# Moving one block's query work: its start put three experts earlier, two contraction steps behind each expert

## The chip, the cores and the metric

The program runs on one core of one Trainium2 chip. The metric is device time in microseconds (us) of one execution. The kernel before takes 1707.67 us (median of 3 runs, 1706.31 to 1708.52). A core has a matrix engine (PE; its weight load is PEld), a vector engine (DVE), a scalar engine (ACT), a general engine (POOL, which here issues the indirect gathers) and SP, which issues the other transfers. All data are float32.

## What is computed

One step of a hybrid decoder for 512 prompt tokens and 64 sample tokens: a token mixer (windowed attention and a spatial gate), a cross attention to memory tokens, and a mixer that picks experts by product keys. The last one takes nearly all of the time. Per token and head it is, cut to what matters:

```python
q = (xt @ w_pq).reshape(PEER_BLOCK, PEER_HEADS, 2, D_HALF)
s = jnp.einsum('thcd,hckd->thck', q, sub_keys)
s1, i1 = lax.top_k(s[:, :, 0], 16)
s2, i2 = lax.top_k(s[:, :, 1], 16)
cand = s1[..., :, None] + s2[..., None, :]          # 16 x 16 pairs
top, sel = lax.top_k(cand, 16)
idx = take_along_axis(i1 * 128 + i2, sel)
gate = softmax(top)
h = einsum('td,thkd->thk', xt, u_tab[idx])
a = gelu(h) * gate
out = einsum('thk,thkd->td', a, v_tab[idx])
```

With 16384 experts of 1024 + 1024 numbers each, every token reads 8 x 16 rows of 8 KB from memory.

## The kernel before

The 576 rows of tokens (64 sample tokens as tile 0, then four tiles of 128) times 8 heads are cut into 36 **blocks** of 128 (token, head) pairs: blocks 0 to 3 hold tile 0 with two heads each, blocks 4 to 11 the first prompt tile, and so on. A block has 16 **experts**, one chosen row per partition each. They are numbered g = 16 x block + k, from 0 to 575; block 4 begins at g = 64.

An expert passes through five engines:

- POOL gathers its 128 rows of 8 KB (1.05 MB) into one of the slots of scratch memory (line 641). Each slot goes round: the gather waits until the expert that held the slot before has been used by PE (`v_used`). A table in the kernel (`SLOT_PHASES`) says which slots take part. Worked out from it, for the experts that the text speaks of: gather 48 takes the slot of expert 40, gather 53 that of 45, 58 that of 50, 64 that of 56, 65 that of 57, 66 that of 58, and 70 that of 63. Before the first gather of a block POOL also waits for that block's indices (`idx_ready`).
- DVE takes the dot product with the tokens (line 1462), once the gather has landed.
- ACT does three small operations (lines 911, 915 and 920): Gelu, times the gate, and a diagonal matrix of the result. Here they are called the diagonal of expert g.
- PE multiplies the diagonal with the second half of the gathered rows into accumulators (line 2009), and so frees the slot.

Each engine's program is one loop over g, in which other work is written between the experts by tables of numbers. An engine never skips an item that has to wait; everything behind it waits too. Two kinds of this other work matter here.

**Query work of a block** (`query_steps`): a counter `step` runs from the block's `query_at` on, one step an expert. Steps 0 to 7 are the 8 contraction steps of the query projection on PE (line 1802), at step 9 ACT copies the sum (`queries_out`, line 811) and PE transposes it (1812), at 11 ACT copies that (815) and PE computes the scores (1823), at 13 ACT copies them (821), at 15 and 16 DVE takes the 16 best of each half (`top_keys`, lines 1284 to 1288), at 18 the 16 best pairs (`best_pairs`, 1302 to 1305), at 20 the expert indices (`experts_of`, 1309 to 1324, after which POOL may gather for that block), at 21 ACT computes the exponentials of the gates (826), at 23 DVE scales them (1329). For a block s `query_at` is (s - 2) x 16, plus `LATE`. For a block in `QUICK` steps 0 to 7 come two at a time behind four experts, and all later steps four experts sooner.

**Units** (`UNIT_AT`): the windowed attention of the prompt tiles 2 to 4, in six pieces u = 0 to 5 that begin at experts 24, 31, 38, 44, 51 and 57. Offsets count from that start: PE scores at 0 (1958), DVE maxima at 4 (1397 to 1404), ACT exponentials at 5 (891), PE transposes at 6 (1971), ACT copies at 8 (897), PE values at 9 (1978), DVE scaling at 12 (1416). Of the odd ones ACT takes a sum of squares and a root at 13 (902, 903), DVE scales the rows at 16 (1268, 1269), PE transposes at 18 (1831) and DVE takes that at 21 (`attn_take`, line 1274). The transposes of unit 3 (at expert 50) wait for the `attn_take` that belongs to unit 1 and stands in DVE's program at expert 52; those of unit 5 (at expert 63) for that of unit 3, at expert 65.

At experts 77 and later the output projection and the next tile's work follow. SP reloads two tiles of the prompt (2 x 512 KB) when expert 59 has been used.

Of the kernel before, what the change touches and what calls it, by code (L numbers as in the profile page):

```python
# [110 lines left out]
def hybrid_step(nc, I, O):  # L111
    ctx = ExitStack()
    with ctx:
# [307 lines left out]
        UNIT_AT = (24, 31, 38, 44, 51, 57)  # L421
        OUT_AT = (77, 81, 85, 91, 95, 99, 105, 109, 113, 119, 123, 127)

        LATE = {4: 8, 12: 7}
        QUICK = (12,)

        def query_at(s):

            return (s - 2) * TOPK + LATE.get(s, 0)

        def query_steps(g):

            steps = []
            for s in range(BLOCKS):
                d = g - query_at(s)
                if s in QUICK and 0 <= d < KD // 2:
                    steps += [(s, 2 * d), (s, 2 * d + 1)]
                elif s in QUICK and KD // 2 <= d < 2 * TOPK:
                    steps.append((s, d + KD // 2))
                elif s not in QUICK and 0 <= d < 2 * TOPK:  # L440
                    steps.append((s, d))
# [1632 lines left out]
```

## Time and profile before

| | |
|---|---|
| time, median of 3 runs | 1707.67 us |
| the profiled execution's own time | 1707.81 us |
| its span | 1706.0 us |
| busy: PE, DVE, ACT, POOL | 1301.5, 1165.7, 810.4, 641.3 us |
| DMA queue of the gathers | 604.28 MB, 85.7% of 16 engines |
| mean over the span | 385 GB/s |
| first and last gather issued | 206.0 and 1676.0 us |

The profile is one execution. Its span leaves out 1.8 us of the execution's own time. A slice of the span (42.65 us each) shows 408 GB/s in the eighth, 374 in the ninth and 420 or more in most others.

### The profile page before, as it was taken

Reading aid. Unit: us, or ns where it says so; the run is one execution under the profiler, and the core shown is the slowest. Engines: PE = TensorE matmul, PEld = TensorE weight load, DVE = VectorE, ACT = ScalarE, POOL = GpSimd, SP = SyncE. Lnnn points to the kernel's source line nnn. Section 1 sums busy time; section 2 is a strip of 40 time slices with the busy share of each in tenths; the row PEclk is TensorE's granted clock in tenths of the full one; section 3 lists DMA queues with packets and bytes.
Section 4 is the critical chain, followed back from the end, with each engine's and each line's share of the span. In section 5 each row is a group of like instructions: output and inputs, shape, how many; then the busy total and the mean of one; then the engine's idle time right before and its main releaser. Section 6 shows DMA issues by size and latency. Waiting matters only on the chain.

```text
span 1706.0 us, 21619 instructions
## 1 busy us (share of the span) xinstructions
PE 1301.5 (76%) x7069; PEld 475.1 (28%) x7069; DVE 1165.7 (68%) x2795; ACT 810.4 (48%) x2337; POOL 641.3 (38%) x584
## 2 busy tenths in 40 slices
PE   9999878987889776677777776776767677667665
PEld 4455523433444222122322111111111111111110
DVE  2544578887667677787777777777667677677764
ACT  1434366775444354455555454445444445444443
POOL 0000044434434344444444443444444444444441
PEclk9999998899999988899988777878888877888866
DMA  9433699999999999999999999999999999999995
GB/s 353 168 138 134 232 400 422 408 374 422 421 421 421 420 398 420 421 403 421 419 421 412 422 421 421 421 422 421 421 421 421 421 405 422 421 421 420 422 419 220
DMA packets 99041, 657.35 MB, mean 385 GB/s; under 512 B 12576, under 2 KB 17568, under 8 KB 22368
## 3 DMA queue, kind: packets, MB, share of 16 engines
q0 software_dynamic: 83056, 604.28, 85.7%
q1 hardware_dynamic: 15872, 51.68, 8.1%
q8 instruction: 56, 0.92, 0.2%
q14 instruction: 57, 0.47, 0.1%
HBM read 652.71 MB, written 4.19 MB: 385 GB/s over the span
## 4 chain that ended last, share of the span: by engine, by line
DMA 44%; PE 26%; ACT 11%; DVE 10%; issue 7%; POOL 2%; ACTq 0%; DVEq 0%; SPq 0%; POOLq 0%
DMA R<-in_peer_uv,R 43%; PE ps L2009 10%; PE ps L1543 6%; DVE R L1462 4%; PE ps L1802 3%; ACT L911 2%; ACT R L920 2%; PE ps L1515 2%; ACT R L915 1%; POOL R L641 1%; ACT R L911 1%; ACT L826 1%; DVE R L1285 1%; DVE R L1286 1%; DVE R L1288 1%
## 5 line engine op out<-in xcount | busy, mean ns | idle before, releaser
L2009 PE MATMUL ps<-R 64*64 64x512 f32 x4536 | 732.3, 725 | 370.4 <-ACT R L920 364.9
L641 POOL DMA_INDIRECT R<-in_peer_uv,R x567 | 627.8, 1107 | 966.4 <-PE ps L2009 762.8
L1462 DVE CUSTOM_DVE_ANT_0 R<-R 128x1024 f32<-128x1024 f32 x567 | 689.3, 1225 | 382.4 <-DMA R<-in_peer_uv,R 368.3
L911 ACT ACTIVATE R<-R 128x1 f32<-128x1 f32 x576 | 115.9, 201 | 594.6 <-DVE R L1462 585.2
L2009 PEld LDWEIGHTS ps<-R 64*64 64x64 f32 x4536 | 134.5, 149 | 713.3 <-ACT R L920 627.1
L920 ACT ACTIVATE R<-R 128x64 f32<-128x64 f32 x576 | 200.4, 348 | 54.3 <-ACT R L915 1.5
L1802 PE MATMUL ps<-A,R 128*128 128x256 f32 (+1 forms) x640 | 224.8, 479 | 0.7 <-ACT R L802 0.7
L915 ACT ACTIVATE R<-R 128x1 f32<-128x1 f32 x576 | 169.8, 295 | 21.2 <-ACT R L911 0.4
L1802 PEld LDWEIGHTS ps<-A,R 128*128 128x128 f32 (+1 forms) x640 | 96.3, 201 | 261.9 <-issue 260.4
L1543 PE MATMUL ps<-A,R 128*128 128x512 f32 (+1 forms) x256 | 101.1, 547 | 0.0
L911 ACT ACT_TABLE_LOAD x60 | 77.0, 1283 | 9.0 <-DVE R L1462 8.0
L1515 PE MATMUL ps<-R 128*128 128x256 f32 (+2 forms) x352 | 78.7, 377 | 0.0
L1515 PEld LDWEIGHTS ps<-R 128*128 128x128 f32 x352 | 60.1, 200 | 23.2 <-issue 16.1
L1543 PEld LDWEIGHTS ps<-A,R 128*128 128x128 f32 x256 | 47.6, 191 | 43.7 <-issue 41.8
L1462 DVE DVE_READ_ACCUMULATOR2_ANT R<- 128x1 f32 x576 | 47.6, 83 | 0.0
L826 ACT ACT_TABLE_LOAD x35 | 44.9, 1283 | 0.6
L1287 DVE MAX8 R<-R 128x8 f32<-128x128 f32 (+1 forms) x108 | 36.7, 339 | 3.7
L1284 DVE MAX8 R<-R 128x8 f32<-128x128 f32 (+1 forms) x108 | 36.3, 336 | 1.9 <-ACT R L821 0.5
L1285 DVE FIND_INDEX8 R<-R 128x8 uint32<-128x128 f32 (+1 forms) x108 | 35.6, 330 | 0.0
L1288 DVE FIND_INDEX8 R<-R 128x8 uint32<-128x128 f32 (+1 forms) x108 | 35.6, 330 | 0.0
L1286 DVE MATCH_REPLACE8 R<-R 128x128 f32<-128x128 f32 (+1 forms) x108 | 34.6, 320 | 0.0
L1823 PEld LDWEIGHTS ps<-R 128*128 128x128 f32 (+1 forms) x160 | 22.0, 209 | 38.2 <-issue 36.6
(288 smaller groups left out, 936.6 us busy)
## 6 DMA issues: line engine op xcount, KB each, us to landing
R<-in_peer_uv,R POOLq DMA_INDIRECT x567
A<-in_w_pq SPq DMA_DIRECT2D x8, 1024.0 KB, 10.3
A<-in_w_in SPq DMA_DIRECT2D x3, 2048.0 KB, 20.5
R<-in_w_out SPq DMA_DIRECT2D x5, 1024.0 KB
x_res<-in_x_prompt SPq DMA_DIRECT2D x6, 512.0 KB, 12.9
R<-in_w_out SPq DMA_DIRECT2D x1, 3072.0 KB
R<-in_x_promptT SPq DMA_DIRECT2D x4, 512.0 KB, 9.2
R<-in_w_cq SPq DMA_DIRECT2D x2, 1024.0 KB, 10.9
```

What stands on the lines that cost most here:

```text
L641: pool.indirect_dma_start(slots[slot_of[g]], None, I["peer_uv"][:, :], bass.IndirectOffsetOnAxis(ap=idx[:, b % 4, k:k + 1], axis=0)).then_ ...
L826: act.activation(gate[:, m, :], bestv, ACT.Exp, bias=negtop, accum_out=esum).then_inc(gexp_ready, 1)
L911: act.activation(hgelu[:, b % 2, col], hdot[:, b % 2, col], ACT.Gelu).then_inc(gelu_ready, 1)
L915: act.activation(coef[:, b % 2, col], gate[:, b % 4, col], ACT.Copy, scale=hgelu[:, b % 2, col])\
L920: act.activation(diag[:, g % DIAGS, :], fold[:, 0:HALF], ACT.Copy, scale=coef[:, b % 2, col])\
L1285: chain(dve.max_index(inds[:, 0:8], vals[:, 0:8], values))
L1288: return dve.max_index(inds[:, 8:16], vals[:, 8:16], values)
L1462: dve.tensor_tensor_reduce(u, u, xn(t), 1.0, 0.0, ALU.mult, ALU.add, hdot[:, b % 2, k:k + 1]).then_inc(u_used, 1)
L1515: ins = pe.matmul(out, lhs(k), rhs(k), start=(k == 0), stop=(k == n - 1))
L1543: ins = pe.matmul(bank(c)[:, 0:CHUNKS[c][1] - CHUNKS[c][0]], tile_T(t)[:, k, :], w_in[c][:, k, :], start=(k == 0), stop=(k == KD - 1))
L1802: ins = pe.matmul(bank(4)[rows, 0:256], expert_T(t)[:, k, :], w_pq(h)[:, k, :], start=(k == 0), stop=(k == KD - 1))
L2009: ins = pe.matmul(bank(2 * (t % 2) + q)[rows], diag[tokens, g % DIAGS, :], v_rows[slot_of[g]][tokens, c * 512:(c + 1) * 512], start=first, ...
```

## The change

```diff
-        LATE = {4: 8, 12: 7}
-        QUICK = (12,)
+        LATE = {4: 5, 12: 7}
+        QUICK = (4, 12)
```

`query_at(4)` goes from 40 to 37, and block 4 joins the blocks whose contraction steps come in pairs. So its steps 0 to 7 stand behind experts 37 to 40 instead of 40 to 47, and each later step stands seven experts sooner: the ACT copies at 42, 44 and 46 instead of 49, 51 and 53; top keys at 48 and 49 instead of 55 and 56; best pairs at 51 instead of 58; indices at 53 instead of 60; the gates' exponentials at 54 instead of 61. The work of no other block moves, the number and kind of instructions stay, and POOL's and SP's programs are the same.

PE's program around experts 37 to 40. L2009 is an expert, L1958 the scores of unit 2, L1978 the values of unit 1, L1802 a contraction step of block 4's queries:

```order
 L2009 MATMUL ps<-R 64x512 x4
+L1802 MATMUL ps<-A,R 128x256 x2
 L1958 MATMUL ps<-R 128x256 x4
-L2009 MATMUL ps<-R 64x512 x8
+L2009 MATMUL ps<-R 64x512 x4
+L1802 MATMUL ps<-A,R 128x256 x2
+L2009 MATMUL ps<-R 64x512 x4
+L1802 MATMUL ps<-A,R 128x256 x2
 L1978 MATMUL ps<-R 128x64 x8
 L2009 MATMUL ps<-R 64x512 x4
-L1802 MATMUL ps<-A,R 128x256
```

Six contraction steps now stand ahead of expert 40, where none stood; two more follow it.

ACT's program of the changed kernel around expert 42. L911, L915 and L920 are a diagonal, L891 and L893 the exponentials of unit 2, L811 the copy of block 4's queries and L815 that of their transpose:

```order
L915 ACTIVATE R<-R 128x1
L920 ACTIVATE R<-R 128x64
L811 ACTIVATE gather<-ps 128x256
L911 ACTIVATE R<-R 128x1
L915 ACTIVATE R<-R 128x1
L920 ACTIVATE R<-R 128x64
L911 ACTIVATE R<-R 128x1
L915 ACTIVATE R<-R 128x1
L920 ACTIVATE R<-R 128x64
L891 ACT_TABLE_LOAD
L891 ACTIVATE R,stat<-R,stat 128x256 x4
L893 ACTIVATE stat<-stat 128x4
```

L811, which stood ahead of the diagonal of expert 49, now stands ahead of that of 42, and with it ahead of unit 2's exponentials.

DVE's program around experts 51 and 52 (the L1462 of x_res and the next one). L1302 to L1305 are block 4's best pairs:

```order
 L1462 ISA x_res,R<-x_res,R 128x1024
 L1462 ISA R 128x1
+L1302 TENSOR_TENSOR R<-R 128x256
+L1284 MAX R<-R 128x8
+L1285 MAX_INDEX R<-R 128x8
+L1286 MATCH_REPLACE R<-R 128x256
+L1287 MAX R<-R 128x8
+L1288 MAX_INDEX R<-R 128x8
+L1305 TENSOR_SCALAR stat<-R 128x1
 L1462 ISA R<-R 128x1024
 L1462 ISA R 128x1
```

Best pairs now stand ahead of expert 52, behind which L1274 (`attn_take`) comes.

## Rows read from the trace of the kernel before

**Rows 1.** The page's DMA queue of the gathers: packets, MB, share of 16 engines.
```profile
q0 software_dynamic: 83056, 604.28, 85.7%
```

**Rows 2.** Windows: length, busy of PE, PEld, DVE, ACT, POOL, PE clock, DMA, GB/s.
```profile
320.00:340.00 20.00, 19.42 (x126) 8.73 (x125) 14.05 (x43) 16.33 (x45) 9.96 (x10) 0.93 1.01 422
...
370.00:372.00 2.00, 0.00 (x0) 0.00 (x0) 1.93 (x6) 1.86 (x4) 0.00 (x0) 0.64 0.85 356
372.00:374.00 2.00, 1.75 (x8) 0.50 (x12) 1.90 (x6) 1.88 (x7) 0.15 (x1) 0.50 0.18 74
374.00:376.00 2.00, 2.00 (x13) 0.38 (x5) 2.00 (x8) 1.86 (x5) 1.70 (x2) 0.50 0.27 49
376.00:378.00 2.00, 2.00 (x13) 2.00 (x13) 1.90 (x10) 1.71 (x5) 1.17 (x2) 0.66 0.88 303
```

**Rows 3.** POOL timeline, gathers 48, 53, 58, 63, 64, 70: start, us, idle before.
```profile
327.87 0.94 POOL L641 DMA_INDIRECT R<-in_peer_uv,R  x1 [1.58 <-PE ps L2009]
...
338.20 0.94 POOL L641 DMA_INDIRECT R<-in_peer_uv,R  x1 [1.37 <-PE ps L2009]
...
352.05 1.69 POOL L641 DMA_INDIRECT R<-in_peer_uv,R  x1 [3.87 <-PE ps L2009]
...
363.53 1.31 POOL L641 DMA_INDIRECT R<-in_peer_uv,R  x1 [0.71 <-PE ps L2009]
373.85 1.13 POOL L641 DMA_INDIRECT R<-in_peer_uv,R  x1 [9.02 <-DVE R L1324]
...
391.01 0.94 POOL L641 DMA_INDIRECT R<-in_peer_uv,R  x1 [6.72 <-PE ps L2009]
```

**Rows 4.** DVE timeline, experts 48 to 59: start, us, line, operation, idle before.
```profile
336.30 1.23 DVE L1462 CUSTOM_DVE_ANT_0 R<-R 128x1024 f32<-128x1024 f32 x1 [0.56 <-DMA R<-in_peer_uv,R]
...
348.44 0.69 DVE L1274 TENSOR_TENSOR R<-ps,gains 128x512 f32<-128x512 f32 x1
...
355.55 0.30 DVE L1284 MAX8 R<-R 128x8 f32<-128x128 f32 x1
...
357.40 0.42 DVE L1397 CUSTOM_DVE_ANT_0 R<-ps,band 128x256 f32<-128x256 f32 x1
...
359.42 1.23 DVE L1462 CUSTOM_DVE_ANT_0 R<-R 128x1024 f32<-128x1024 f32 x1
...
365.10 0.42 DVE L1302 TENSOR_TENSOR R<-R 128x256 f32<-128x256 f32 x1
...
368.18 1.22 DVE L1462 CUSTOM_DVE_ANT_0 x_res<-x_res,R 128x1024 f32<-128x1024 f32 x1
```

**Rows 5.** PE timeline, experts 40 to 64.
```profile
325.98 1.09 PE L2009 MATMUL ps<-R 64*64 64x512 f32 x8
327.00 0.70 PE L1802 MATMUL ps<-A,R 128*128 128x256 f32 x2
...
336.81 1.09 PE L2009 MATMUL ps<-R 64*64 64x512 f32 x8 [0.58 <-ACT R L920]
...
349.27 1.07 PE L1971 MATMUL ps<-ident,R 128*128 128x128 f32 x8 [1.81 <-DVE R L1274]
350.65 1.09 PE L2009 MATMUL ps<-R 64*64 64x512 f32 x8 [0.31 <-ACT R L920]
...
372.25 1.98 PE L2009 MATMUL ps<-R 64*64 64x512 f32 x8 [3.04 <-ACT R L920]
...
387.22 1.57 PE L1971 MATMUL ps<-ident,R 128*128 128x128 f32 x8 [4.67 <-DVE R L1274]
```

**Rows 6.** ACT timeline, experts 42 to 49.
```profile
322.35 0.20 ACT L911 ACTIVATE R<-R 128x1 f32<-128x1 f32 x1 [0.27 <-DVE R L1462]
...
326.51 1.28 ACT L891 ACT_TABLE_LOAD   x1
...
334.18 0.29 ACT L903 ACTIVATE stat<-stat,eps 128x1 f32<-128x1 f32 x1
...
343.59 0.38 ACT L811 ACTIVATE gather<-ps 128x256 f32<-128x256 f32 x1 [3.15 <-PE ps L1802]
```

## The prediction

> **What bounds the kernel now.** I read the page's DMA queues first: the gathers bring 604.28 MB and take 85.7% of the engines' span [rows 1]. One gather is 604.28 / 576 = 1.049 MB, which at the full rate of 422 GB/s [rows 2] is 2.49 us. While that stream is full, the end waits for nothing else; time is lost only where it runs dry. So I looked next, in the windows, for where it does, and found one place near the change: 356, 74, 49 and 303 GB/s in the four windows from 370 to 378 [rows 2]. The shortfall is (66 + 348 + 373 + 119) x 2 / 422 = 4.3 us; the stream stands from about 371.8 to 376.0, and I carry 4.2 us. The POOL timeline tells why: gather 64 is issued at 373.85, 10.3 us behind gather 63, after 9.02 us of waiting for line 1324, the last instruction of block 4's indices [rows 3]. That is the wait the change moves. Data begin 2.15 us behind the start of an issue (373.85 to 376.0).
>
> From this comes a yardstick. Gather n must be issued by 371.8 - 2.49 x (64 - n) - 2.15, or the stream runs dry: 329.8 for gather 48, 342.3 for 53, 354.7 for 58, 369.7 for 64. Before they come at 327.87, 338.20 and 352.05 [rows 3], so the margins are 1.9, 4.1 and 2.7 us. They are small, and they are what the change spends. The rest of the reading was of the three engine timelines between 320 and 391: who is behind whom, and what stands behind a waiting item.
>
> **The part that goes.** Indices of block 4 stand seven experts sooner, so they no longer hold gather 64. Its slot is free when expert 56 is done; if nothing else moved, the 4.2 us would go.
>
> **The part that is added, on PE.** A contraction step takes 0.63 us (327.00 to the next expert [rows 5]; the row's 0.70 overlaps it). Six of them now stand ahead of expert 40, 3.8 us of work on an engine that is already late there: PE starts expert 40 at 325.98 [rows 5], while ACT is at diagonal 42 at 322.35 [rows 6]. So expert 40 starts at 329.8 and ends at 330.8, and its two steps end at 332.1. Gather 48 comes at 331.1, 1.3 us past its yardstick.
>
> **The wait that is added, on ACT.** The copy of the queries (line 811) stands ahead of diagonal 42 and needs the last contraction step. ACT gets there at about 322.3 and stands until 332.1, nearly 10 us. Before, the same copy stood at diagonal 49 and cost 3.15 us [rows 6]. Behind the waiting copy are diagonals 42 and 43 and unit 2's exponentials (line 891), and for them wait DVE at expert 46 and PE's transposes at expert 44. Copy and two diagonals of 0.87 us each bring ACT to the exponentials at 332.1 + 0.4 + 1.7 = 334.2 instead of 326.51 [rows 6], 7.7 us late. From there to 340.4 (343.59 less the 3.15 us of waiting) ACT had no wait, so all of that lateness is kept: expert 45, which PE starts at 336.81 as soon as its diagonal is there [rows 5], starts at 344.5 and ends at 345.5. Gather 53 comes at 345.8, 3.5 us past its yardstick.
>
> **What DVE makes of it.** It takes the scaling of unit 1's rows only after ACT's root (line 903, 334.18 [rows 6], now 7.7 later and done at 342.2), and so starts expert 48 at 342.8 instead of 336.30 [rows 4]. It ends it at 343.9 and waits for the copied scores until 344.9. Then comes a run in which it has no more slack, and into which block 4's selection is put: top keys 1.85 (355.55 to 357.40), maxima of unit 3 2.0 (357.40 to 359.42), expert 49 1.15, top keys 1.85, experts 50 and 51 with a 0.4 us scaling 2.7, best pairs 3.1 (365.10 to 368.18), expert 52 1.15 [all rows 4]. Sum 13.8: line 1274 starts at 358.7 and ends at 359.4, where it started at 348.44 [rows 4]. 6.8 us of the 13.8 are the moved selection, the rest of the delay is ACT's.
>
> PE's transposes of unit 3 wait for line 1274 [rows 5]. They start at 359.4 instead of 349.27, and expert 50, which started at 350.65 [rows 5], 10 us later, ending at 361.3 or so. Gather 58 comes at 361.6, where the yardstick is 354.7: the stream has lost 6.9 us by then. This holds the losses at gathers 48 and 53, since a yardstick is passed once and not added.
>
> **Behind that.** DVE now has no best pairs and indices at 58 and 60, which gives back 5.7 us. Expert 56 is done near 374, gather 64 comes at about 374.2, 4.5 past its yardstick, which is less than 6.9; so it costs nothing new, and the indices, ready near 363, cost nothing either. The second place of the same kind is gather 70. Its yardstick is 387.1, with the 2.49 us of the reloaded prompt tiles, plus what was lost before. In the kernel before it comes at 391.01 [rows 3], just within 387.1 + 4.2. PE there waited 4.67 us for the next line 1274 [rows 5]; carried through, DVE is 4 to 5 us later at it, and gather 70 comes at 394 to 395, 6.9 to 7.9 past. I take 6.9.
>
> **The clock.** After a wait of 3.04 us PE runs an expert in 1.98 instead of 1.09 us [rows 5], at a granted clock of 0.50, the 1.2 GHz level [rows 2]; after 4.67 us a set of transposes takes 1.57 instead of 1.07 [rows 5]. The changed kernel has waits of about 3 us ahead of experts 44 and 45 and one of about 6 ahead of 50. Nothing says that each brings the low clock (after 1.81 us it stayed up [rows 5]), so the cost up to gather 58 lies between 0 and 3.8 us: 0.5 + 0.9 for the transposes and expert 50, and two experts and a unit at twice their time before, 2.4. I take 2.5, nearer to the rows that have a wait as long. The Trainium skill ("TensorE: Matmul & The Clock Gate", "Why this matters for your kernels") says that idle gaps between bursts of matmuls bring the engine back to half rate. By that rule, the trace agrees, and every one of the three waits would pay: 3.8 instead of 2.5.
>
> The sum: 6.9 + 2.5 - 4.2 = +5.2 us. The profiled execution took 1707.81 us, 0.1 above the median of 1707.67; 1707.8 + 5.2 = 1713.0.
>
> The Trainium skill ("DMA: Bandwidth & Descriptors", "Latency and other measured facts") gives about 1 us to the first byte of a transfer that POOL issues. This trace shows 2.15 us. With the page's figure every yardstick lies 1.15 us later, the new loss is 8.25 instead of 9.4, and the sum would be +4.0, 1711.9; the trace decides.
>
> **Rivals.**
> Faster: the stretch has room for the moved work. DVE is busy for only 14.05 of the 20 us from 320 to 340 [rows 2], so part of the 6.8 us of selection fits into its waits. It decides at gather 58: if the delay there stays under its margin of 2.7 us, nothing is lost ahead of 64. Then gather 64 comes by 369.7, gather 66 at 374.3 within 374.6, and nearly all of the 4.2 goes: 1703.6 to 1704.8. Against it stands the order: ACT cannot pass line 811 before PE has done eight steps, and PE was behind before any was added. 1 in 10.
>
> About the same: the chain is as told, but half of ACT's lateness is absorbed, because PE's added steps fill waits of its own, and because expert 50 is late by 6 us and not by 10. Then the loss is 4 to 5 us for the 4.2 that go: 1707.5 to 1709. 17 in 100.
>
> Slower than forecast, by the clock: each wait of the chain brings the low level, the slower PE lets ACT and DVE wait again, and the loss grows beyond gather 58 to 12 or 14 us: 1715.5 to 1718. The idle times of 3.04 and 4.67 us with their slow rows [rows 5] speak for it, that DVE and not PE sets expert 50 against it. 18 in 100.
>
> That the change does nothing is excluded: line 811 stands in another place of ACT's program.
>
> **Numbers.** The forecast itself has 55 in 100, with a range of its own of 1709.5 to 1715.5. About 0.2% (3.4 us) is what a measurement of this kernel can tell from no change. Slower by more than that, above 1711.1, are the clock's 0.18, 0.52 of the forecast's 0.55 and 0.02 of the third case: 0.72. Within 0.2% are 0.15 of that case and 0.03 of the forecast: 0.18. Faster is 0.10. The range for 8 in 10 leaves out the faster rival and the far end of the clock's: 1706.8 to 1718.0.
>
> **What would show it.** In the changed kernel: line 811 at expert 42 with 8 to 10 us of waiting for line 1802, near 332; the exponentials of unit 2 near 334; gather 53 near 346; top keys of block 4 from 345, best pairs near 354; line 1274 near 359 and PE's transposes waiting for it by 5 us or more; no wait of POOL for line 1324 near block 4; and windows under 400 GB/s near gathers 53 and 58 (347 to 364), with none around gather 64. From gather 71 on everything stands 4 to 7 us later than before. I am wrong if ACT's wait at line 811 is under 5 us, or if gather 58 comes by 357, or if the stream makes up time behind gather 70.

## The result, and the profile of the changed kernel

The changed kernel takes 1715.93 us (median of 6 runs, 1713.49 to 1721.76), the one before 1707.59 us (6 runs). The ratio is 1.0052, with a 95% interval of 1.0039 to 1.0065: 8.3 us slower. The forecast was 1713.0, +5.2. By the interval the change costs 6.7 to 11.1 us. On another chip, beside other kernels, the ratio was 1.0040 (1.0027 to 1.0053), 4.6 to 9.1 us.

The windows show where the gathers' stream ran dry, and the whole stretch of 100 us (columns as in [rows 2]). The changed kernel:

```profile
330.00:332.00 2.00, 1.69 (x14) 0.41 (x16) 2.00 (x3) 1.51 (x6) 1.77 (x1) 1.00 0.69 283
332.00:334.00 2.00, 2.00 (x18) 0.41 (x10) 0.12 (x2) 1.94 (x3) 1.62 (x2) 1.00 0.81 225
346.00:348.00 2.00, 2.00 (x22) 1.38 (x25) 1.90 (x8) 0.64 (x2) 0.54 (x1) 1.00 0.79 238
360.00:362.00 2.00, 2.00 (x9) 0.39 (x3) 1.90 (x6) 1.86 (x6) 0.01 (x1) 0.50 0.31 131
362.00:364.00 2.00, 2.00 (x14) 1.01 (x17) 2.00 (x3) 1.97 (x4) 1.83 (x1) 0.95 0.00 0
364.00:366.00 2.00, 2.00 (x18) 0.51 (x10) 1.90 (x13) 1.83 (x6) 0.94 (x1) 1.00 0.75 193
398.00:400.00 2.00, 2.00 (x10) 0.50 (x2) 1.97 (x5) 0.61 (x3) 1.23 (x2) 0.57 0.75 193
320.00:420.00 100.00, 78.14 (x510) 35.76 (x510) 73.49 (x210) 69.44 (x187) 39.67 (x36) 0.93 0.94 365
```

The kernel before in the same 100 us:

```profile
320.00:420.00 100.00, 83.75 (x538) 37.67 (x537) 77.16 (x216) 72.08 (x198) 43.24 (x39) 0.92 0.97 402
```

The old gap between 372 and 376 [rows 2] is gone. Only from 361.5 to 364.5 does the stream now stand still, but it runs thin near 332, near 347, near 371 and from 398 to 410 as well. Over the stretch the shortfall against 422 GB/s is (422 - 365) x 100 / 422 = 13.5 us: 3.1 up to 340, 1.8 from 346 to 352, 4.5 from 360 to 366, 1.1 from 368 to 376 and 3.0 from 398 to 410. Before, it is (422 - 402) x 100 / 422 = 4.7 us. The difference is 8.8 us. The 20 us ahead of the stretch go the other way (422 GB/s for 393 before), so that 7.4 us are left, which is how much later gathers 91 to 100 are issued (7.6 us). The last gather is issued 8.25 us later than before (1684.23 for 1675.98).

Gathers 48, 53, 58, 64 and 70 in the POOL timeline, which answer to [rows 3]:

```profile
329.99 1.78 POOL L641 DMA_INDIRECT R<-in_peer_uv,R  x1 [3.38 <-PE ps L2009]
...
344.36 0.94 POOL L641 DMA_INDIRECT R<-in_peer_uv,R  x1 [3.56 <-PE ps L2009]
...
361.99 1.85 POOL L641 DMA_INDIRECT R<-in_peer_uv,R  x1 [9.67 <-PE ps L2009]
...
375.44 1.26 POOL L641 DMA_INDIRECT R<-in_peer_uv,R  x1 [1.21 <-PE ps L2009]
...
397.75 0.94 POOL L641 DMA_INDIRECT R<-in_peer_uv,R  x1 [7.09 <-PE ps L2009]
```

POOL no longer waits for line 1324 ahead of gather 64. It waits 9.67 us for PE ahead of gather 58, which comes 9.9 us later than before and 7.3 past its yardstick of 354.7.

ACT, which answers to [rows 6]:

```profile
330.28 0.38 ACT L811 ACTIVATE gather<-ps 128x256 f32<-128x256 f32 x1 [8.75 <-PE ps L1802]
...
332.40 1.28 ACT L891 ACT_TABLE_LOAD   x1
...
361.76 1.28 ACT L826 ACT_TABLE_LOAD   x1
```

The copy of the queries now stands ahead of diagonal 42 and waits 8.75 us; behind it unit 2's exponentials begin at 332.40 instead of 326.51.

DVE, which answers to [rows 4]. The rows are the first top keys, best pairs, line 1274 for unit 1, the indices, and line 1274 for unit 3:

```profile
343.22 0.30 DVE L1284 MAX8 R<-R 128x8 f32<-128x128 f32 x1 [0.72 <-ACT R L821]
...
352.76 0.42 DVE L1302 TENSOR_TENSOR R<-R 128x256 f32<-128x256 f32 x1
...
357.00 0.68 DVE L1274 TENSOR_TENSOR R<-ps,gains 128x512 f32<-128x512 f32 x1
...
361.67 0.18 DVE L1324 SCALAR_TENSOR_TENSOR R<-R 128x16 uint32<-128x16 f32 x1
...
392.76 0.68 DVE L1274 TENSOR_TENSOR R<-ps,gains 128x512 f32<-128x512 f32 x1
```

And PE, which answers to [rows 5] (the row of 330.17 is expert 41, that of 342.97 experts 45 and 46, the last one experts 63 and 64):

```profile
330.17 1.09 PE L2009 MATMUL ps<-R 64*64 64x512 f32 x8
...
342.97 2.22 PE L2009 MATMUL ps<-R 64*64 64x512 f32 x16 [2.77 <-ACT R L920]
...
357.83 1.94 PE L1971 MATMUL ps<-ident,R 128*128 128x128 f32 x8 [6.12 <-DVE R L1274]
359.70 1.99 PE L2009 MATMUL ps<-R 64*64 64x512 f32 x8
...
393.59 1.94 PE L1971 MATMUL ps<-ident,R 128*128 128x128 f32 x8 [4.65 <-DVE R L1274]
395.46 3.69 PE L2009 MATMUL ps<-R 64*64 64x512 f32 x16
```

PE's transposes of unit 3 wait 6.12 us for line 1274, and with expert 50 behind them they run at half speed (1.94 for 1.07 us, 1.99 for 1.09), while the granted clock is 0.50.

### The profile page after: what moved, and what is told of

It reads as the page before. It is cut to its first block, busy times and chain, and to the rows that moved or that the text cites. A ratio compares the mean times of both kernels' runs of the same rounds, so it can differ in the third digit from the quotient of the medians.

```text
span 1713.4 us, 21618 instructions
## 1 busy us (share of the span) xinstructions
PE 1308.2 (76%) x7069; PEld 476.8 (28%) x7069; DVE 1165.6 (68%) x2795; ACT 809.8 (47%) x2337; POOL 642.1 (37%) x584
## 4 chain that ended last, share of the span: by engine, by line
DMA 45%; PE 23%; DVE 12%; ACT 11%; issue 7%; SPq 1%; POOL 1%; ACTq 0%; DVEq 0%; POOLq 0%
DMA R<-in_peer_uv,R 43%; PE ps L2009 9%; DVE R L1462 4%; PE ps L1543 4%; PE ps L1802 3%; ACT L911 2%; ACT R L920 2%; PE ps L1515 2%; ACT R L915 2%; DMA R<-in_mem_prompt 1%; DVE R L1285 1%; ACT R L911 1%; DVE R L1286 1%; DVE R L1288 1%; ACT L826 1%
## 5 line engine op out<-in xcount | busy, mean ns | idle before, releaser
L2009 PE MATMUL ps<-R 64*64 64x512 f32 x4536 | 739.4, 732 | 365.3 <-ACT R L920 364.8
L1462 DVE CUSTOM_DVE_ANT_0 R<-R 128x1024 f32<-128x1024 f32 x567 | 689.0, 1225 | 378.5 <-DMA R<-in_peer_uv,R 371.8
L911 ACT ACTIVATE R<-R 128x1 f32<-128x1 f32 x576 | 115.9, 201 | 599.5 <-DVE R L1462 598.4
L2009 PEld LDWEIGHTS ps<-R 64*64 64x64 f32 x4536 | 134.9, 150 | 717.9 <-ACT R L920 640.6
L920 ACT ACTIVATE R<-R 128x64 f32<-128x64 f32 x576 | 200.4, 348 | 54.3 <-ACT R L915 1.9
L1802 PE MATMUL ps<-A,R 128*128 128x256 f32 (+1 forms) x640 | 221.5, 472 | 0.7 <-ACT R L802 0.7
L915 ACT ACTIVATE R<-R 128x1 f32<-128x1 f32 x576 | 169.8, 295 | 21.1 <-ACT R L911 0.4
L1802 PEld LDWEIGHTS ps<-A,R 128*128 128x128 f32 (+1 forms) x640 | 95.9, 199 | 259.2 <-issue 256.8
L1462 DVE DVE_READ_ACCUMULATOR2_ANT R<- 128x1 f32 x576 | 47.3, 82 | 0.0
L811 ACT ACTIVATE gather<-ps 128x256 f32<-128x256 f32 x36 | 13.5, 375 | 39.8 <-PE ps L1802 39.8
```

The lines of the kernel that those rows point to most:

```text
L911: act.activation(hgelu[:, b % 2, col], hdot[:, b % 2, col], ACT.Gelu).then_inc(gelu_ready, 1)
L915: act.activation(coef[:, b % 2, col], gate[:, b % 4, col], ACT.Copy, scale=hgelu[:, b % 2, col])\
L920: act.activation(diag[:, g % DIAGS, :], fold[:, 0:HALF], ACT.Copy, scale=coef[:, b % 2, col])\
L1462: dve.tensor_tensor_reduce(u, u, xn(t), 1.0, 0.0, ALU.mult, ALU.add, hdot[:, b % 2, k:k + 1]).then_inc(u_used, 1)
L1802: ins = pe.matmul(bank(4)[rows, 0:256], expert_T(t)[:, k, :], w_pq(h)[:, k, :], start=(k == 0), stop=(k == KD - 1))
L2009: ins = pe.matmul(bank(2 * (t % 2) + q)[rows], diag[tokens, g % DIAGS, :], v_rows[slot_of[g]][tokens, c * 512:(c + 1) * 512], start=first, ...
```

## The experiments

Each kernel was run in 5 rounds beside the kernel before. Single executions there differ by 3 to 7 us either way, so the ratios count. A time in a profile of one execution is read beside the first gather of the same profile, which begins between 203.5 and 208.7 us (206.04 before). The last three experiments were run on another chip than the others.

### The changed kernel again

> The changed kernel as it is, on the chip of the other runs of this call, since single executions there differ by 3 to 4 us either way: both theories +6 to +10 us against before. It is the measure for the three beside it.

1.0040 (1.0027 to 1.0053), +6.8 us. The rows are those of the first profile within 0.2 us: the copy waits 8.68 us, PE waits 6.13 for line 1274, gather 58 comes at 361.97.

### Only sooner, and only in pairs

```diff
-        LATE = {4: 8, 12: 7}
+        LATE = {4: 5, 12: 7}
```

> Block 4 three experts sooner, still one contraction step an expert. Theory (the copy's wait on ACT makes the loss, and it is long because PE had eight steps less time): ACT now meets the copy at expert 46, five experts after the changed kernel's 42 minus one; by then PE has caught up in part, the wait is 3 to 6 us instead of 8.75, and the time is +0 to +4 us against before. Rival (pairs make no difference, the loss comes from the selection standing three to seven experts sooner, ahead of line 1274): here the best pairs stand at 55, behind line 1274 at 52, so it would give the full gain, -3 to -4 us. A second rival, the loss comes with the date alone: +6 to +8 us, as in the changed kernel.

1.0004 (0.9993 to 1.0014). The copy waits only 1.21 us. Gather 64 needs no index any more, but PE waits 4.07 us for line 1274, and gather 70 comes 4.0 us later than before, both counted from the first gather: the old gap's time is spent again. Neither rival came.

```diff
-        QUICK = (12,)
+        QUICK = (4, 12)
```

> Pairs of contraction steps behind experts 40 to 43, copy at 45, selection at 51, 52, best pairs 54, indices 56; the start is not sooner. Theory: PE has finished its slow stretch before expert 40 and unit 1's values, so the copy waits 3 to 6 us and not 8.75; about -1 to +3 us against before, clearly under the +8.3 of both parts together. Rival (the pairs are the cause by themselves): +5 us or more.

1.0006 (0.9992 to 1.0020). The copy waits 0.76 us; PE waits 5.66 us for line 1274. So neither half costs what both cost, +0.7 and +1.0 us, neither clear of zero, for +8.3: the loss belongs to the place where both bring the block. That the copy waits hardly at all in either was not expected (3 to 6 us were).

### How far down the chain

Here the first of block 4's steps stand where the changed kernel has them, and the later ones where the kernel before has them. Contraction steps alone:

```diff
+                if s == 4:
+                    steps += [(s, n) for n in range(2 * TOPK) if (37 + n // 2 if n < 8 else 40 + n) == g]
+                    continue
```

> Only PE's eight contraction steps stand where the changed kernel has them (behind experts 37 to 40, in pairs); copies, scores, selection and gates stand where before has them. Theory: PE's added work ahead of expert 40 costs little, since ACT does not wait for it: within 1 us of before, and POOL waits for line 1324 as before (about 9 us). Rival (PE's late experts 40 and 41 and so gathers 48 and 49 are the cause): +3 us or more.

1.0016 (1.0005 to 1.0026), +2.7 us. The forecast of "within 1 us" missed, and the rival, PE's late experts and the gathers behind them (+3 us or more), is inside the interval (0.9 to 4.4 us). The added lines move the numbers by three, so line 1274 is L1277 and 1971 is L1974 in PE's rows:

```profile
354.58 1.94 PE L1974 MATMUL ps<-ident,R 128*128 128x128 f32 x8 [5.39 <-DVE R L1277]
...
394.30 1.94 PE L1974 MATMUL ps<-ident,R 128*128 128x128 f32 x8 [4.91 <-DVE R L1277]
```

ACT does not wait for PE's contraction steps here. Counted from the first gather, gather 48 comes 3.1 us later than before, line 1274 2.6 us later and gather 58 4.0 us later. No part of the selection stands ahead of line 1274 here: DVE comes to it late because the gathered rows of the experts ahead land late (it waits 1.88 and 1.25 us for them). PE's wait for it grows from 1.81 [rows 5] to 5.39 us, and the transposes fall to half speed.

Contraction steps, copies and scores as changed, selection and gates as before:

```diff
+                if s == 4:
+                    steps += [(s, n) for n in range(2 * TOPK) if (37 + n // 2 if n < 8 else 33 + n if n < 15 else 40 + n) == g]
+                    continue
```

> Contraction steps, copies, transposes and scores of block 4 where the changed kernel has them (copy at expert 42), but the selection on DVE and the gates where before has them (top keys 55, best pairs 58, indices 60). Theory (ACT's wait is the first cause, the selection ahead of line 1274 about doubles it at gather 58): wait of 8 to 9 us at the copy, line 1274 at 349 to 353 instead of 357.0, and +2 to +5 us against before, between nothing and the changed kernel's +8.3. Rival A (ACT's wait alone makes it): +7 us or more. Rival B (the selection alone makes it): 0 to +1 us.

1.0035 (1.0019 to 1.0051), +6.0 us, more than the +2 to +5 expected. The copy on ACT, line 1274 on DVE (here L1277) with PE's transposes behind it, and gather 64 on POOL:

```profile
332.12 0.38 ACT L814 ACTIVATE gather<-ps 128x256 f32<-128x256 f32 x1 [9.54 <-PE ps L1805]
```

```profile
355.87 0.69 DVE L1277 TENSOR_TENSOR R<-ps,gains 128x512 f32<-128x512 f32 x1
```

```profile
356.70 1.06 PE L1974 MATMUL ps<-ident,R 128*128 128x128 f32 x8 [1.98 <-DVE R L1277]
```

```profile
379.50 1.14 POOL L644 DMA_INDIRECT R<-in_peer_uv,R  x1 [6.84 <-DVE R L1327]
```

It pays twice: ACT's wait of 9.54 us makes the stream lose ahead of gather 53, and the indices, which DVE still takes at expert 60, hold gather 64 as before. Rival B, the selection alone, is refuted; rival A, ACT's wait alone (+7 us or more), is not (the interval is 3.2 to 8.7 us). The forecast for line 1274 was 349 to 353, and it comes at 355.87: counted from the first gather that is only 0.3 us sooner than in the changed kernel, with none of the moved selection ahead of it. The copy comes 2.7 us later here, so the 6.8 us of selection delay line 1274 by about 3 us and not by 6.8. The rest of the selection falls into waits that DVE has without it. (The profiled execution, 1719.24 us, was 3.5 above this kernel's median.)

### Taking one link out of the changed kernel

Everything behind the contraction steps three experts later, so that the copy stands at 45 and has nothing to wait for:

```diff
-                elif s in QUICK and KD // 2 <= d < 2 * TOPK:
-                    steps.append((s, d + KD // 2))
+                elif s in QUICK and KD // 2 + 3 * (s == 4) <= d < 2 * TOPK + 3 * (s == 4):
+                    steps.append((s, d + KD // 2 - 3 * (s == 4)))
```

> The changed kernel with everything of block 4 behind the contraction steps three experts later: contraction pairs behind 37 to 40 as changed, copy on ACT at 45, transpose copy 47, scores 49, top keys 51 and 52, best pairs 54, indices 56. Theory (ACT's wait at the copy is the first cause): the copy waits under 1 us, unit 2's exponentials start within 3 us of before (326.5), gather 53 comes within 2 us of before, and the time is 0 to +4 us against before, at least 4 us better than the changed kernel. Rival (the selection ahead of line 1274, wherever the copy stands): one set of top keys still stands ahead of it, none of the best pairs, so a third of the loss, +2 to +3. Rival (PE's steps ahead of expert 40 are the cause): no better than +6.

1.0026 (1.0015 to 1.0037), +4.4 us, 2.4 better than the changed kernel on the same chip where at least 4 were expected. ACT's wait at the copy is gone altogether. The start of each of the two sets of top keys and line 1274 on DVE, PE's transposes of unit 3, and gather 58:

```profile
348.18 0.29 DVE L1284 MAX8 R<-R 128x8 f32<-128x128 f32 x1
...
351.16 0.29 DVE L1284 MAX8 R<-R 128x8 f32<-128x128 f32 x1
...
353.00 0.69 DVE L1274 TENSOR_TENSOR R<-ps,gains 128x512 f32<-128x512 f32 x1
```

```profile
353.84 1.94 PE L1971 MATMUL ps<-ident,R 128*128 128x128 f32 x8 [5.68 <-DVE R L1274]
```

```profile
357.99 0.94 POOL L641 DMA_INDIRECT R<-in_peer_uv,R  x1 [8.92 <-PE ps L2009]
```

So with no wait on ACT at the copy more than half of the loss is left: PE is late by itself, both sets of top keys (3.7 us of the 6.8 us of selection, not one set as the expectation has it) stand ahead of line 1274, and PE waits 5.68 us for it. This edit also takes the best pairs from ahead of line 1274, so it does not price ACT's wait alone.

Line 1274 two experts sooner in both places, for unit 1 at expert 50, ahead of the best pairs, and for unit 3 at 63, with ACT's wait left in:

```diff
-                elif step == 21 and r == 1:
+                elif step == 19 and r == 1:
                     attn_take(t)
```

> The changed kernel with DVE's attn_take (line 1274) two experts sooner: at expert 50 for unit 1 and at 63 for unit 3, ahead of block 4's best pairs and not behind them. It takes the wait of PE for it away and leaves ACT's wait as it is. Theory (two links: ACT's wait, then the selection ahead of line 1274): PE's transposes of unit 3 wait under 2 us instead of 6.1, gather 58 comes near 357 instead of 362, gather 53 as late as in the changed kernel; part of the loss moves on to gathers 65 and 66, since ACT stays late: +3 to +6 us against before. Rival (ACT's wait alone makes the loss): no change from +8. Rival (line 1274 alone makes it): 0 to +1 us.

1.0009 (1.0000 to 1.0018), +1.5 us (0.0 to 3.1), beside +6.8 of the changed kernel on the same chip. PE, and gathers 58, 64 and 65:

```profile
354.02 1.04 PE L1971 MATMUL ps<-ident,R 128*128 128x128 f32 x8
```

```profile
356.38 0.94 POOL L641 DMA_INDIRECT R<-in_peer_uv,R  x1 [0.77 <-PE ps L2009]
...
371.65 0.94 POOL L641 DMA_INDIRECT R<-in_peer_uv,R  x1 [1.75 <-PE ps L2009]
378.33 1.16 POOL L641 DMA_INDIRECT R<-in_peer_uv,R  x1 [5.74 <-PE ps L2009]
```

The transposes no longer wait for DVE and keep full speed, gather 58 comes 5.6 us sooner (4.6 beside the first gather), and what is left shows at gather 65, as expected. The gain was larger than the +3 to +6 expected of it, and the rival that line 1274 alone makes the loss (0 to +1 us) is inside the interval. The same move in the kernel before changes nothing (below), so 5.3 of the 6.8 us hang on the place of line 1274. But ACT's wait is part of what makes line 1274 late: the links stand one behind the other, and their prices do not add up.

### Is there a gain in the old gap?

The changed kernel's aim was that gap. One expert sooner, nothing else (`LATE = {4: 7, 12: 7}`):

> Not the changed kernel: the one before with block 4 one expert sooner (start at 39), one contraction step an expert. Theory (what the old gap costs can be had back as long as nothing of ACT or DVE is made to wait): indices about 2.5 us sooner, contraction ends one expert sooner for a copy that waited 3.15 us, so that wait stays: -2.5 to +0.5 us. Rival (the stretch is so full that any sooner date loses): +1 to +4 us.

0.9997 (0.9986 to 1.0007). Gathers 64 and 70:

```profile
370.74 0.94 POOL L641 DMA_INDIRECT R<-in_peer_uv,R  x1 [7.05 <-DVE R L1324]
...
391.14 0.94 POOL L641 DMA_INDIRECT R<-in_peer_uv,R  x1 [6.62 <-PE ps L2009]
```

Gather 64 comes 3.1 us sooner than before, gather 70 at 391.14 as before (391.01 [rows 3]): it is held by PE's wait for the second line 1274, and the time gained is waited away six gathers on. The copy on ACT waits 0.77 us here and not the 3.15 that were expected to stay.

The move of line 1274 alone, in the kernel before:

> The kernel before with line 1274 two experts sooner (50 and 63 instead of 52 and 65), block 4 where it was. Theory (gather 70 is held by PE's wait of 4.67 us for line 1274, and behind the gap at gather 64 it has 0.3 us to spare): the wait goes, gather 70 comes 1 to 4 us sooner, but the gap ahead of gather 64 stays, so the time does not move: -1.5 to +1 us. Rival (line 1274 costs before too): -3 us or more.

0.9997 (0.9986 to 1.0008). The profile's first gather is 2.4 us later than before, and gather 64 is held by the indices as it was; gather 70, counted from the first gather, comes 2.8 us sooner, as expected:

```profile
376.96 1.14 POOL L641 DMA_INDIRECT R<-in_peer_uv,R  x1 [9.02 <-DVE R L1324]
...
390.60 0.94 POOL L641 DMA_INDIRECT R<-in_peer_uv,R  x1 [4.09 <-PE ps L2009]
```

Both together:

> Line 1274 two experts sooner and block 4 one expert sooner (start at 39, one contraction step an expert). One expert sooner alone brought gather 64 3.1 us forward and left gather 70 at 391.1 and the time at -0.5 +/- 1.8 us. Theory (both hold the stream, one behind the other): together -2 to -4 us, gather 64 near 370.7, gather 70 under 390. Rival (the gap at gather 64 was hidden anyway and costs nothing): within 1 us of before.

0.9981 (0.9970 to 0.9992), 1705.73 us: 3.2 us faster than the kernel before (1709.05 there), and the one version that is faster than both kernels clear of the noise. Gathers 64 and 70, and PE's transposes of unit 5:

```profile
372.01 0.94 POOL L641 DMA_INDIRECT R<-in_peer_uv,R  x1 [8.83 <-DVE R L1324]
...
389.05 1.63 POOL L641 DMA_INDIRECT R<-in_peer_uv,R  x1 [2.92 <-PE ps L2009]
```

```profile
385.38 1.09 PE L1971 MATMUL ps<-ident,R 128*128 128x128 f32 x8 [1.36 <-ACT stat L893]
```

The transposes, which waited 4.67 us for DVE [rows 5], wait 1.36 us for ACT and keep the full speed. Counted from the first gather, gather 64 comes 1.3 us and gather 70 1.5 us sooner than before. The 80 us that begin 134 us behind the first gather (340 to 420 in the kernel before) show the two places together:

| version | GB/s in these 80 us | short of 422 GB/s |
|---|---|---|
| before | 397 | 4.7 us |
| one expert sooner | 399 | 4.4 us |
| line 1274 sooner | 393 | 5.5 us |
| both | 409 | 2.5 us |
| two experts and line 1274 sooner (next experiment) | 399 | 4.4 us |

So only with both moves does the stream lose less there. These are single profiles, and the difference in time between both moves and line 1274's alone is 2.7 us, give or take 2.7: that the two places work together is likely and not shown.

Two experts sooner and line 1274 sooner (`LATE = {4: 6, 12: 7}`):

> As the one beside it, with block 4 two experts sooner (start at 38). The indices stand at expert 58 and come near 367, within the yardstick of gather 64 (369.7), so nothing of the old gap is left; the copy on ACT stands at 47, where PE is still behind. Theory: -2 to -4 us if the copy waits under 3 us; 0 to -1 if it waits longer and gather 53 or 58 passes its yardstick.

0.9995 (0.9983 to 1.0007), -0.9 us. The copy waits for nothing, so the expectation of -2 to -4 missed, though the profiled execution was the shortest, with a span of 1701.0 us. What this step loses again was not followed up.

## Why the prediction was right, and where its sum was short

**The yardstick and the old gap.** Right. The old gap went, and POOL's wait for line 1324 with it. But what it is worth was taken too simply: one expert sooner freed 3.1 us at gather 64 and nothing in time; with line 1274 sooner as well it was 3.2 us. One reading behind the yardstick is rough. The stream of the kernel before stands still from 373.25, and its data begin at 375.50, 1.65 us behind the start of the issue and not 2.15; then it runs thin:

```profile
373.25:375.50 2.25, 2.25 (x16) 0.44 (x8) 2.18 (x7) 2.11 (x7) 1.34 (x2) 0.50 0.00 0
375.50:376.75 1.25, 1.25 (x8) 0.88 (x5) 1.22 (x9) 1.24 (x3) 0.95 (x2) 0.50 0.82 170
```

So the 2.15 us stand for first data at 1.65 us and a slow stretch behind them; as a delay in the yardstick they serve, as the time to the first data they are 0.5 us too long.

**PE's steps ahead of expert 40.** Expert 41 starts at 330.17, and the steps end near 330.2, 1.9 us sooner than the 332.1 of the sum. A pair of steps takes 1.06 us (323.22 to 324.28) and not 2 x 0.63, which is 0.6 us of it. Gather 48 comes at 329.99 and not 331.1, only 0.2 past its yardstick. Yet the stream lost 3.1 us by 340, half of it from 330 to 334. That these steps cost by themselves, 2.7 us by experiment, the prediction did not have; it held that a loss at gather 48 is contained in the later one at gather 58.

**ACT's wait.** Expected nearly 10 us until 332.1, measured 8.75 until 330.28; exponentials at 332.4 for 334.2; gather 53 at 344.36 for 345.8. Right in kind, with dates 1.4 to 1.8 us too late.

**DVE and line 1274.** The run of 13.8 us was right: from the top keys at 343.22 to line 1274 at 357.00 it is 13.8 us (the start had been put at 344.9 and 358.7). But the split of it, 6.8 us of selection and the rest ACT's, does not hold: with the copies as changed and the selection where it was, line 1274 comes 0.3 us sooner, or about 3 us for a copy at the same time. Of the two experiments with a link out, the one without ACT's wait at the copy (and without the best pairs ahead of line 1274) keeps +4.4 us, the one without the wait for line 1274 keeps +1.5 us.

**Gather 58.** 361.99 for the forecast 361.6. That is luck: two errors cancel. It would have been 1.8 us sooner but for the clock, which the sum of 6.9 left out and carried as a term of its own.

**The clock.** Put at 2.5 us up to gather 58, at three waits. The waits ahead of experts 44 and 45 (1.87 and 2.77 us) left the granted clock at 1.00. The one of 6.12 us was followed by 0.50: 0.87 + 0.90 = 1.8 us up to gather 58. After the second wait for line 1274 (4.65 us) transposes and experts 63 and 64 take 1.94 and 3.69 us, where they took 1.57 [rows 5] and 3.07 before: 1.0 us more. Of this only the 0.4 of the transposes stands ahead of gather 70, which is issued 2.29 us behind the start of expert 63 in both kernels. So 1.8 to 2.2 us reached the stream, near the 2.5 in size, and at other places. The Trainium skill ("TensorE: Matmul & The Clock Gate", "Why this matters for your kernels") says that gaps between bursts of matmuls bring the half rate. This case's traces agree for the waits of 3.04 [rows 5], 4.65 and 6.12 us and show nothing of it behind those of 1.87 and 2.77. The length of the wait does not settle it. In the kernel before, further on, a shorter one was followed by half speed:

```profile
408.30 1.98 PE L2009 MATMUL ps<-R 64*64 64x512 f32 x8 [2.48 <-ACT R L920]
```

Over that whole trace 23 single experts stand behind a wait of 2 to 3 us; 12 took under 1.2 us, 8 took 1.9 to 2.0, 3 lay between. All 8 behind a wait of 4 us or more took 1.9 to 2.0.

**The sum.** This is the step that was short: 9.4 us of loss were forecast for the stretch, 13.5 are measured, against 4.2 and 4.7 of before. Two terms were mis-sized. Gather 70 comes at 397.75 and not at 394 to 395, 10.65 past its yardstick; the forecast with its clock term had 9.4. That is 1.2 us. And the yardstick counts one loss and takes the later ones to contain it. Measured, 13.5 - 10.65 = 2.8 us are lost beyond it, before 4.7 - 4.2 = 0.5: windows such as 332 to 334 with 225 GB/s and 346 to 348 with 238, in which a gather comes near its yardstick and the stream runs thin. That is 2.3 us, of which the last gather's 8.25 keeps 1.8. By 366 the stream had lost 9.4 us, where gather 58 is 7.3 past its yardstick. How short the sum of +5.2 us fell is uncertain: it lies under the interval of the first measurement (6.7 to 11.1 us) and inside that of the repeat (4.6 to 9.1, with 6.8 in the middle).

**The rivals.** The faster one failed at its own point: gather 58 was 9.9 us late where 2.7 were allowed. The forecast's own range, 1709.5 to 1715.5, just misses the measured 1715.93, which lies in that of the clock's rival (1715.5 to 1718.0). But the reason that this rival gives is not what happened: not each wait brought the low clock, and of the 3.1 us beyond the forecast the clock explains 0.3 at most. The range for 8 in 10 holds it.

**The signs.** The waits, the dates of the copy, line 1274 and gathers 53 and 58 came within 2 us of what was named, and none of the three signs of being wrong showed. Two signs missed: the stream was thin from 368 to 376 (328 to 381 GB/s), where nothing was expected near gather 64, and behind gather 71 the delay is mostly 7 to 8 us and not 4 to 7.

What is left open: why single executions of the same kernel differ by more on the second chip, what ACT's wait costs by itself, why the losses at the gathers add up beyond the yardstick, and what the start two experts sooner gives back.

## What to carry to other kernels

A stream that is full most of the time gives each stage a date by which it must free a slot; work them out from the rate, and compare the change with the margins (here 1.9 to 4.1 us) and not with the gap it aims at. Moving work to an earlier place costs whatever stands behind it on every engine that it touches: a copy on ACT that waits takes all of ACT's queue along, and moving one small DVE instruction, for which PE waits, out from behind other work gave back 5.3 of the 6.8 us. Such links stand one behind the other: work on one engine that fills a wait it would have had anyway costs less than its own length (here 6.8 us of selection about 3 us). Before closing one gap look for the next instruction that would hold the stream a few items on; here two moves of no measurable worth alone gave 3.2 us together.

## What was not expected of the hardware

The stream loses rate before it runs dry and after it starts again: 2 us windows beside a gather near its yardstick show 225 to 324 GB/s at a DMA share of 0.69 to 0.95, and behind the old gap the first 1.25 us ran at 170. Only 4.5 of the 13.5 us lost lie in the windows from 360 to 366, where it stood still; the other 9 are thin windows. PE's clock kept its full level after waits of 1.87 and 2.77 us in the changed kernel and stood at half after 4.65 and 6.12; in the kernel before a wait of 2.48 us was followed by half speed.
